# Three attention stages of an attention and state-space kernel become one program of 128 units

## The reference, cut to what matters

```python
scale = NSA_HEAD_DIM ** -0.5
# compressed: 63 keys, each from 32 tokens
s = jnp.einsum('bhgtd,bhcd->bhgtc', q, kc).astype(jnp.float32) * scale
p = jax.nn.softmax(jnp.where(valid, s, NEG_BIG), axis=-1)
o = jnp.einsum('bhgtc,bhcd->bhgtd', p.astype(vc.dtype), vc)
# select_blocks: 8 of 16 blocks of 64 keys for each token and group, from p
imp = jnp.einsum('bhgtc,cs->bhts', p_cmp, overlap)
_, idx = lax.top_k(score, min(SEL_TOPK, n_sb))
# selected: softmax attention over the keys of these blocks, with a distance bias
# sliding: softmax attention over the last 512 keys, with a distance bias
o_nsa = g[0] * o_cmp + g[1] * o_slc + g[2] * o_win
```

## Time and profile before

| | us |
|---|---|
| median of 3 runs | 2789.66 |
| lowest and highest | 2789.05, 2793.44 |
| the profiled execution, its own time | 2796.18 |
| its span in the trace | 2794.0 |
| PE busy | 2571.3 (92%) |
| DVE busy | 1428.1 (51%) |
| ACT busy | 1003.6 (36%) |

### The profile page before, as it was taken

How to read it: one execution, slowest core, us unless ns; L and a number is a source line. 1 busy time by engine, 2 the same in 40 slices (tenths; PEclk the granted TensorE clock), 3 DMA queues, 4 the chain that set the end, 5 groups by cost and what they waited for, 6 DMA issues and landing times. The chain is left out here.

```text
span 2794.0 us, 34554 instructions
## 1 busy us (share of the span) xinstructions
PE 2571.3 (92%) x12876; PEld 2119.0 (76%) x12876; DVE 1428.1 (51%) x3114; ACT 1003.6 (36%) x2275; POOL 181.3 (6%) x188
## 2 busy tenths in 40 slices
PE   8999987799997799998989999888799999999998
PEld 6888876677986678876668888666678888888877
DVE  5244256755778764129855722588672223223235
ACT  4223123344675433118852231444442222122132
POOL 2000000000000012002200010342000000000000
PEclk9999976699998999999999999899899999999999
DMA  4112120000000152100011141000541111111113
GB/s 150 31 46 79 57 63 1 1 1 1 2 1 1 55 170 71 48 15 20 24 61 50 47 168 57 31 1 14 186 155 42 48 55 49 49 46 49 50 56 140
DMA packets 105077, 153.04 MB, mean 55 GB/s; under 512 B 35408, under 2 KB 49872, under 8 KB 104912
## 3 DMA queue, kind: packets, MB, share of 16 engines
q1 hardware_dynamic: 96464, 125.67, 14.6%
q0 software_dynamic: 3840, 12.59, 1.1%
q10 hardware_dynamic: 4608, 12.58, 1.1%
HBM read 121.44 MB, written 29.36 MB: 54 GB/s over the span
## 5 line engine op out<-in xcount | busy, mean ns | idle before, releaser
L202 PE MATMUL banks<-mhT,mmwhi 128*128 128x512 f32 x1024 | 316.3, 390 | 3.9 <-ACT qsq L2914 2.8
L193 PE MATMUL banks<-mmwhi,fT 128*128 128x512 f32 x1024 | 316.1, 390 | 3.7 <-ACT qsq L2914 3.7
L193 PE MATMUL banks<-g1whi,hT 128*128 128x512 f32 (+1 forms) x1024 | 304.5, 381 | 7.8 <-ACT gates L428 3.0
L177 DVE TENSOR_TENSOR mmwlo<-mmwraw,mmwhi 128x512 fp32r<-128x512 f32 x144 | 97.2, 690 | 368.1 <-ACT mmwhi L172 368.0
L172 ACT ACTIVATE mmwhi<-mmwraw 128x512 fp32r<-128x512 f32 x144 | 89.2, 630 | 412.7 <-DMA mmwraw<-in_w_down 206.7
L193 PEld LDWEIGHTS banks<-mmwhi,fT 128*128 128x128 f32 x1024 | 191.9, 188 | 45.2 <-ACT qsq L2914 5.4
L202 PEld LDWEIGHTS banks<-mhT,mmwhi 128*128 128x128 f32 x1024 | 191.7, 188 | 45.2 <-ACT qsq L2914 4.1
L193 PEld LDWEIGHTS banks<-g1whi,hT 128*128 128x128 f32 x1024 | 189.1, 190 | 45.3 <-issue 4.3
L193 PE MATMUL banks<-mmwlo,fT 128*128 128x512 f32 x512 | 199.5, 390 | 0.0
L202 PE MATMUL banks<-mhT,mmwlo 128*128 128x512 f32 x512 | 199.5, 390 | 0.0
L193 PE MATMUL banks<-g1wlo,hT 128*128 128x512 f32 (+1 forms) x512 | 194.6, 380 | 0.0
(11 more groups left out here) (438 smaller groups left out, 5403.6 us busy)
## 6 DMA issues: line engine op xcount, KB each, us to landing
mmwraw<-in_w_up SPq DMA_DIRECT2D x64, 256.0 KB, 2.7
mmwraw<-in_w_down SPq DMA_DIRECT2D x64, 256.0 KB, 2.6
g1wraw<-in_w_in SPq DMA_DIRECT2D x56, 256.0 KB, 2.7
g3wraw<-in_w_in SPq DMA_DIRECT2D x40, 256.0 KB, 2.6
qx<-x_scratch SPq DMA_DIRECT2D x16, 512.0 KB, 6.2
xt<-in_x SPq DMA_DIRECT2D x8, 512.0 KB, 5.3
z_scratch<-zst POOLq DMA_DIRECT2D x16, 256.0 KB, 4.1
cw<-in_cmp_w SPq DMA_DIRECT2D x2, 2048.0 KB, 10.0
```

Of the source, the lines that this page charges most:

```text
L177: self.nc.vector.tensor_tensor(self.lo[n][:, c], self.raw[n][:, c], f32(self.hi[n][:, c]), ALU.subtract)\
L193: ins = self.nc.tensor.matmul(out, l, r[:, c], start=k == 0 and i == 0, stop=k == self.nk[j] - 1 and i == 2)
L202: ins = self.nc.tensor.matmul(out, l[:, col], r, start=k == 0 and i == 0, stop=k == self.nk[j] - 1 and i == 2)
```

## The change

`cmp_stage` and the two calls of `attention_stage` go; `nsa_stage` stands in their place as one `nc.Block()`. It has the same 128 units, in another order: long tiles first, sliding (WIN) and selected (SEL) alternating, and at the end groups of three, one long selected unit and two short ones. The work of the compressed attention is cut into steps (S scores, F and F2 bias and maximum, E exponential, N division, I, I2 and I3 ranking, T transposes, O values, Z transposed mask, G gate), and each step of a query tile is issued behind a given unit's turn. All chunks of weights, and the masks, are copied by ACT. Scores are issued up to three units ahead (before: two), over the same four banks, which the compressed scores now share (one bank of the four for a step S). The compressed attention has one buffer `sc` where it had two. The instructions of a unit are those of before, except for the engine of the odd copies. The gated sum in `o_nsa` is a plain product for whoever is first at its place and an addition for those after; where the compressed output isn't first (tiles 7 and 6), it takes two instructions instead of one.

```diff
-def cmp_stage(nc, sem, mem, C, qT, kcT_hi, kcT_lo, vbd, gates, o_nsa, selT, psum, kb):
...
+def nsa_stage(nc, sem, mem, C, qT, kcT_hi, kcT_lo, vbd, kT, v, gates, o_nsa, selT, psum2, psum, x_kb, pt_kb, stat_kb,
...
+    XR, H, SEL, WIN = 4, NSA_HEADS, 1, 2
+
+    def group(branch, t):
+        return [(branch, t, h) for h in range(H)]
+
+    units = []
+    for branch, t in ((WIN, 7), (WIN, 6), (SEL, 7), (SEL, 6), (WIN, 5), (WIN, 4), (WIN, 3), (SEL, 3), (WIN, 2), (SEL, 2)):
+        units += group(branch, t)
+    long_units = group(SEL, 5) + group(SEL, 4)
+    short_units = group(WIN, 1) + group(SEL, 1) + group(WIN, 0) + group(SEL, 0)
+    for i in range(2 * H):
+        units += [long_units[i], short_units[2 * i], short_units[2 * i + 1]]
+    NU = len(units)
+    x = [mem.at("nsx", x_kb + 4 * i, [P, SEQ], F32) for i in range(XR)]
+    pt = [mem.at("nspt", pt_kb + 2 * i, [P, 4, P], F32) for i in range(4)]
+    st = mem.at("nsst", stat_kb, [P, 4, 16], F32)
+    sc = mem.at("csc", stat_kb + 0.5, [P, H, 64], F32)
...
+    OFFSET = {"S": 0, "F": 0, "F2": 1, "E": 2, "N": 3, "I": 4, "I2": 4, "I3": 5, "T": 5, "O": 6, "Z": 7, "G": 7}
+    FIRST = dict(OFFSET, T=8, O=9, G=10)
+    BASE = {c: 0 if c == NT - 1 else 10 + (6 * (NT - 2 - c) + 1 if c < NT - 2 else 0) for c in range(NT)}
+
+    def at(step, u):
+
+        for c in range(NT):
+            if BASE[c] + (FIRST if c == NT - 1 else OFFSET)[step] == u:
+                return c
...
+    for u in range(NU):
+        mine = [("unit", u, c, min(4, tiles_of(u) - c)) for c in range(0, tiles_of(u), 4)]
+        of_unit.append(range(len(chunks), len(chunks) + len(mine)))
+        chunks += mine
...
+    s = 0
+    for u in range(-1, NU):
+        now = []
+        while s < NU and s <= u + 3:
+            prior = [user[m] for m in banks_next(keys(s) > 512) if m in user]
+            if any(kind == "unit" and i > u for kind, i in prior):
+                break
+            place(("unit", s), keys(s) > 512)
+            now.append(s)
+            s += 1
+        issue.append(now)
+        if at("S", u) is not None:
+            place(("cmp", at("S", u)), False)
...
+                released(pe, ("unit", u))
+                if selected(u) and h == 0:
+                    pe.wait_ge(copied, chunks.index(("Z", t, 0, 0)) + 1)
...
+            def turn_chunk(c):
+                kind, w, k, n = chunks[c]
+                if c >= 2:
+                    pe.wait_ge(copied, c - 1)
+                bank = psum[4 + c % 2]
+                if kind == "unit":
+                    for i in range(n):
+                        last = nc.tensor.transpose(bank[:, tile(i)], x[w % XR][:, tile(k + i)], C["ident"][:])
+                elif kind == "T":
+                    pe.wait_ge(c_p, n_cmp[w] + 1)
...
+            def out_bank(o):
+                if o >= 2:
+                    pe.wait_ge(o_done, o - 1)
+                return psum[6 + o % 2]
...
+            for u in issue[0]:
+                scores(u)
+            for u in range(NU):
+                for n in issue[u + 1]:
+                    scores(n)
+                pe.wait_ge(e_ready, u + 1)
+                for c in of_unit[u]:
+                    turn_chunk(c)
+                if u >= 1:
+                    values(u - 1)
+                if at("O", u) is not None:
+                    cmp_values(at("O", u))
+                for c in after_unit[u]:
+                    turn_chunk(c)
+                if at("S", u) is not None:
+                    cmp_scores(at("S", u))
+            values(NU - 1)
...
+                if kind == "Z":
+                    dst = selT[:, w - 4, :, :]
+                    src = psum[4 + c % 2][0:N_SEL, 0:2 * P].rearrange("p (v q) -> p v q", v=NSA_KV)
+                else:
+                    last = [consumer(i) for i in range(c % 4, c, 4) if consumer(i) is not None]
+                    if last:
+                        act.wait_ge(o_ready, last[-1])
+                    n = 4 if kind == "T" else n
+                    dst, src = pt[c % 4][:, 0:n, :], psum[4 + c % 2][:, 0:n * P].rearrange("p (k q) -> p k q", k=n)
...
+            for u in range(NU):
+                act.wait_ge(m_ready, u + 1)
+                nc.scalar.activation(x[u % XR][:, 0:keys(u)], x[u % XR][:, 0:keys(u)], ACT.Exp,
+                                     bias=st[:, 0, u % 16:u % 16 + 1], scale=-1.0,
+                                     accum_out=st[:, 1, u % 16:u % 16 + 1]).then_inc(e_ready, 1)
+                if u >= 1:
+                    for c in of_unit[u - 1]:
+                        copy_chunk(c)
+                    for c in after_unit[u - 1]:
+                        copy_chunk(c)
+                c = at("E", u)
+                if c is not None:
+                    act.wait_ge(c_x, n_cmp[c] + 1)
+                    nc.scalar.activation(sc[:], sc[:], ACT.Exp).then_inc(c_e, 1)
...
+                dve.wait_ge(s_ready, u + 1)
+                if u >= XR:
+                    dve.wait_ge(t_ready, of_unit[u - XR][-1] + 1)
+                nc.vector.tensor_tensor_reduce(out=x[u % XR][:, 0:n], in0=score_bank(("unit", u), 0, n),
+                                               in1=table[:, width - n:], scale=-2.0 ** -(h + 1), scalar=3e38,
+                                               op0=ALU.add, op1=ALU.min, accum_out=st[:, 0, u % 16:u % 16 + 1])\
+                    .then_inc(m_ready, 1)
...
+            def output(u):
+                branch, t, h = units[u]
+                a, o = u % 16, outs["unit", u]
+                dve.wait_ge(e_ready, u + 1)
+                ch.link(nc.vector.reciprocal(st[:, 2, a:a + 1], st[:, 1, a:a + 1]))
+                ch.link(nc.vector.tensor_tensor(st[:, 3, a:a + 1], st[:, 2, a:a + 1],
+                                                gates[:, t, branch * 8 + h:branch * 8 + h + 1], ALU.mult))
+                dve.wait_ge(o_ready, o + 1)
...
+            def front(c):
+                dve.wait_ge(c_s, n_cmp[c] + 1)
+                if c < NT - 1:
+                    dve.wait_ge(t_ready, chunks.index(("T", c + 1, 0, 0)) + 1)
+                nc.vector.tensor_tensor(sc[:], score_bank(("cmp", c), 0, 512).rearrange("p (h c) -> p h c", h=H),
+                                        C["cslope"][:].to_broadcast(m8), ALU.mult).then_inc(c_in, 1)
+                dve.wait_ge(c_in, n_cmp[c] + 1)
+                cc.link(nc.vector.tensor_tensor(sc[:], sc[:], C["cmask"][:, c:c + 1, :].to_broadcast(m8), ALU.add))
+
+            def front2(c):
+                cc.link(nc.vector.tensor_reduce(cst[:, 0, :], sc[:], AX_X, ALU.max))
+                nc.vector.tensor_tensor(sc[:], sc[:], cst[:, 0, :].unsqueeze(2).to_broadcast(m8), ALU.subtract)\
+                    .then_inc(c_x, 1)
+
+            def norm(c):
+                dve.wait_ge(c_e, n_cmp[c] + 1)
+                cc.link(nc.vector.tensor_reduce(cst[:, 1, :], sc[:], AX_X, ALU.add))
...
+                if before["cmp", c] < 0:
+                    nc.vector.tensor_tensor(rows, src, gate, ALU.mult).then_inc(o_done, 1)
+                else:
+                    dve.wait_ge(t_ready, chunks.index(("T", c, 0, 0)) + 1)
+                    cc.link(nc.vector.tensor_tensor(sc[:], src, gate, ALU.mult))
+                    dve.wait_ge(o_done, before["cmp", c] + 1)
+                    nc.vector.tensor_tensor(rows, rows, sc[:], ALU.add).then_inc(o_done, 1)
...
+            for u in issue[0]:
+                bias_min(u)
+            for u in range(NU):
+                if u >= 2:
+                    output(u - 2)
+                for n in issue[u + 1]:
+                    bias_min(n)
+                for step, work in (("G", gated), ("F", front), ("F2", front2), ("N", norm), ("I", importance),
+                                   ("I2", blocks), ("I3", ranking)):
+                    c = at(step, u)
+                    if c is not None and (step not in ("I", "I2", "I3") or c >= 4):
+                        work(c)
+            output(NU - 2)
+            output(NU - 1)
+
...
-    cmp_stage(nc, sem, mem, C, nqT, kcT[0], kcT[1], vbd, gates, o_nsa, selT, psum, 153)
...
-    attention_stage(nc, sem, "sl", mem, C,
-                    nsa_units(ksT, lambda k, g: kv1[:, k, 384 + g * HD:384 + (g + 1) * HD], 1, lambda t: 0,
-                              C["dist"], True), 1, psum2, psum, 153, 169, 177)
...
-    attention_stage(nc, sem, "wi", mem, C,
-                    nsa_units(kwT, lambda k, g: kv2[:, k, 128 + g * HD:128 + (g + 1) * HD], 2,
-                              lambda t: max(0, t - WINDOW // P), C["wdist"], False), 1, psum2, psum, 153, 169, 177)
+    values = {1: lambda k, g: kv1[:, k, 384 + g * HD:384 + (g + 1) * HD],
+              2: lambda k, g: kv2[:, k, 128 + g * HD:128 + (g + 1) * HD]}
+    nsa_stage(nc, sem, mem, C, nqT, kcT[0], kcT[1], vbd, {1: ksT, 2: kwT}, values, gates, o_nsa, selT, psum2, psum,
```

(25 more changed lines are left out.)

291 lines of the change are left out of this document (168 added, 123 removed).

## The result

The kernel after takes 2758.73 us (median of four runs, 2755.12 to 2760.16) against 2789.94 (2789.05 to 2793.44): a ratio of 0.9884 [0.9868, 0.99]. It is faster, by 31 us. The forecast was 67 us; 2758.73 lies above its range too. A run over 1.5% above the fastest of its kernel counts as slow and stays out of the ratios, which of all the runs here touches one, of the split copies.

The account below looks back on a forecast made before the run. PE was taken as the bound: 269.3 + 26.9 + 2 + 1 + 3 + 5 = 307.2 us for the new stage against 374.4, a gain of 67.2, so 2789.7 - 67.2 = 2722.5 us, range 2708 to 2748.

Parts of the forecast that it names:

- The order in the queues: New stage: compressed steps in DVE's queue and one of four score banks taken by S; stalls and hand-offs of 5 us.
- The clock's term: Start of the new stage: a possible stretch at half clock there costs 3 us.
- Units, 269.3 us: PE's work at full clock on all sliding and selected units of the new stage: 269.3 us.
- compressed work, 26.9: PE's compressed scores 14.2, values 8.3 (0.13 each) and transposes 4.4 us in the new stage: 26.9 us together.
- a group of three with two one-tile units: End of the new stage: one long selected unit and two one-tile units take 3.8 us.
- rival 2: Units of query tiles 0 to 3: ACT alone is the bound, its hand-off exposed, 19 us, 2742 us; chance 0.08.
- start, end and stalls: New stage: start 2 us, draining end 1 us, and stalls with hand-offs 5 us.
- Copies at no cost: New stage: moving DVE's copies to ACT costs nothing on average, hidden under PE.
- The 24 us of before's half-clock starts, hand-offs and drains: Old selected and sliding stages: 293.1 us against 269.3; the 24 us between are half-clock starts, uncovered hand-offs and the drain.
- Rival 1: Compressed steps on DVE delay the biases, some 3 us of PE per tile: +24 us, about 2746; chance 0.16.
- Rival 3: Small PE waits between mixed units hold the stage at 1.2 GHz: 100 us more, 2890, slower kernel; chance 0.03.
- the rule against the change: Skill's advice to empty PSUM with both ScalarE and VectorE; against copies on ACT alone, its sum would be rival 2's.

Follow-up runs that it names:

- the split copies: In the kernel with F later, DVE instead of ACT copies the odd chunks of weights: 2729.38, 2758.05, 2762.29 and 2786.01 us, 0.9849 without the last.
- one early F: In the kernel with F later, tile 4's step F is put back to its early turn: 2756.18 us, 0.9873.
- F later: In the kernel after, step F of every tile stands one turn later, behind the output of the unit before: 2727.77 us, 0.9771.

## Why the prediction was wrong, step by step

With O and G one turn later the time is 2722.66 us, where the forecast was 2722.5. The sum was that of a kernel without the fault, though that it agrees to 0.2 us is luck (step 3); what failed is one step and the term that hangs on it.

1. *"The order in the queues"* is the step that failed. It asked whether DVE's time and the four score banks suffice, and both did. It never listed the two output banks. The 5 us of stalls put there stand against 6.5 us of waits for that bank, so as stalls they would have done no harm.
2. *The clock's term, 3 us, only for the start.* It was wrong both ways. At the start nothing was lost: 1.00 from 435.50 to 527. In the middle 59 + 8 + 8 us ran below 1.00, where I had no term. By the length of the stage in the traces, 345.1 us for the kernel after, 337.7 with one early F, 309.9 with F later and 308.4 with O and G later, the 36.7 us are 27.9 for the first wait with its fall, 7.4 for the others, and 1.5 that F's later turn leaves. By medians the same steps are 28.4, 2.6 and 5.1, but these hold differences outside the stage as well, and the two kernels with F later have the wait at unit 48, which the other two have not.
3. *Units, 269.3 us, and compressed work, 26.9.* The sum held, partly by luck: the kernel with O and G later runs 308.4 us from first score to the next stage, against 308.6. Its parts moved against each other. With the compressed stage apart the units take 799.52 - 518.67 = 280.8 us, with their start, drain and start at half clock, where the forecast had 269.3 + 2 + 1 + 3 and 1.3 for the marks, 276.6. That leaves 27.6 us for the compressed work and its stalls, where it had 31.9. In the kernel after, PE's scores of the compressed tiles go at 0.11 us at full clock, as forecast, and the values too, which I had at 0.13:

```profile
522.26 1.11 PE L1366 MATMUL banks<-vbd,nspt 128*128 128x128 f32 x8
523.12 0.28 PE L1357 MATMUL banks<-kcT,nqT 128*128 128x64 f32 x1
...
524.80 0.28 PE L1358 MATMUL banks<-kcT,nqT 128*128 128x64 f32 x1
```

Eight value instructions (two in the trace for each of the four matmuls of the code) in 523.12 - 522.26 = 0.86 us, 0.11 each: 1.3 us less than the forecast; scores 1.68 us for 15 starts, 0.112 each. Against that, a group of three with two one-tile units takes longer. The same place in two groups that follow each other:

```profile
753.88 0.30 PE L1324 MATMUL banks<-ident,nsx 128*128 128x128 f32 x1 [0.28 <-ACT nspt L1401]
...
758.57 0.30 PE L1324 MATMUL banks<-ident,nsx 128*128 128x128 f32 x1 [0.28 <-ACT nspt L1401]
```

4.69 us where I had 3.8: 7 us in eight groups, and one more in the eight with two-tile units (5.45 where I had 5.3, from 716.11 to 721.56). PE waits 0.28 us for ACT's copy in the former, which is rival 2 in small. The clock's 3 us did not come, and PE's idle time in the kernel with O and G later is 307.00 - 300.33 = 6.7 us in all, the waits in the groups included, where start, end and stalls had 8.
4. *Copies at no cost*: right. *The 24 us of before's half-clock starts, hand-offs and drains*: not won by the new order and the one stage alone. Order, one stage and copies give 2789.9 - 2778.9 = 11 us while the compressed stage stands apart; hiding that stage gives the other 56 (2778.9 to 2722.7). Hiding is 5/6 of the gain, and the clock gained at the start is in it: after the old compressed stage PE stood at 0.50, after "hn" at 1.00.
5. *The rivals.* Rival 1 had the right place, F ahead of other work on DVE, but asked DVE's time for the price and named tiles 7 and 6; the waits came at the S of tiles 4 to 0, and DVE was not full there (it idled 4.31 us ahead of F, and was busy for 205.8 of the stage's 343.5 us). Its 24 us are near the 28 by chance. Rival 3 had the right mechanism, a clock that falls behind a small wait of PE, and asked for it stage-wide and at 100 us. The two belong together: a short wait as trigger, 59 us at half clock as price. I had given the clock's rule 0.03 since PE with gaps held 1.00 from 538 to 542; that row shows that gaps may go unpunished, not that they do. "TensorE: Matmul & The Clock Gate" of the Trainium skill, section "A second HAM failure mode: psum-queue depth-cycling", names frequent small idles between groups of matmuls that cycle through banks as a trigger. The trace agrees in part (1.41 us at a bank wait, and 0.50 behind it): one wait was enough here, and there was no swinging, but 52 us flat at 0.50.

Rival 2 fell: splitting the copies gained nothing in either kernel. The section "PSUM Bottleneck" of "TensorEngine Tiling (Array Packing)" in the Trainium skill gives its advice to empty PSUM with both engines for a TensorE that packing has made faster, which this kernel's is not, so the rule against the change was stretched. The runs do not bear it out for this kernel (2784.91 with ACT alone against 2789.45 in the kernel before).

## What to carry to other kernels

When steps are moved to other turns, list every ring that the moved step shares with others, output banks too, and for each one read in the releasing engine's queue what stands ahead of the release and what that waits for; a count of free time on the engines doesn't find such a wait. Price a wait of 1 to 2 us of a dense PE stream with the clock behind it and with the work that follows it: here it was up to 4 us in two places and 28 in another. To find it, shift one step by one turn: two such kernels told what a whole profile left open.

## What the hardware showed that I had not expected

- One idle of 1.41 us in a PE stream that was busy 88.63 of 92.00 us was followed by 1.2 GHz, and PE, busy 52.00 of 52 us, did not get 2.4 GHz back until other work came (one early F at tile 4).
- With the mask matmuls of 16 rows in the mix it took 57 us to come back, without them some 7, with sliding units behind it 6 to 7. Why is open.
- A wait of such a length is not always followed by a fall (1.24 us in the kernel after, clock 1.00 behind it). With a chain of small waits (up to 2.4 us, the split copies) one and the same program took 2729.38, 2758.05 and 2762.29 us, at a mean clock of 0.973, 0.962 and 0.963.
- The value instructions of 128 columns in float32 started 0.11 us apart at full clock, as the scores of 64 columns did (kernel after, 522 to 525); the trace has two of them for one matmul of the code, so that such a matmul takes 0.22.
